# Building an expert gate table by one-hot matmuls, or by indirect DMA of single elements

## The chip, the cores and the metric

The kernel runs on one core of one Trainium2 chip. The metric is the device time of one execution in microseconds (us). The engines are PE (TensorE, with its weight loads shown apart as PEld), DVE (VectorE), ACT (ScalarE), POOL (GpSimd) and SP (SyncE, which here only issues DMAs).

## The reference

Two transformer blocks are applied to 512 tokens of width 1024, all in float32. The part that matters is the last one, a feed-forward layer over 16,384 experts of one neuron each. For each token and each of 8 heads, two lists of 128 key scores are ranked, the best 16 of each are crossed, and the best 16 of the 256 sums name 16 experts. A softmax over the 16 gives the gates.

```python
s1, i1 = lax.top_k(s[:, :, 0], PEER_TOPK)
s2, i2 = lax.top_k(s[:, :, 1], PEER_TOPK)
cand = (s1[..., :, None] + s2[..., None, :]).reshape(...)
cidx = (i1[..., :, None] * PEER_NKEYS + i2[..., None, :]).reshape(...)
cs, ci = lax.top_k(cand, PEER_TOPK)
eidx = jnp.take_along_axis(cidx, ci, axis=-1)
g = jax.nn.softmax(cs, axis=-1)
hid = jnp.einsum('cd,chkd->chk', xc, ug).astype(jnp.float32)
a = jax.nn.gelu(hid, approximate=False) * g
return jnp.einsum('chk,chkd->cd', a.astype(vg.dtype), vg)
```

A token can pick the same expert in several heads; its gates then add up.

## The kernel before, in words

The program is written by hand: each engine has one instruction stream, and semaphores tie the streams together. The first half of it computes the two attention blocks. The change is in the expert layer, which has two stages.

**Hidden stage.** The 16,384 experts are walked as 128 tiles of 128 experts. For tile e, SP loads a 512 KB weight tile (`load_u`, four slots). Products are made in three passes of a split float32: ACT writes the high part of the weights (`high_u`, two slots), POOL subtracts it from the weights to get the low part (`low_u`), and PE multiplies high by high, high by low and low by high: 24 matmuls of 512 columns per tile (`hidden`). ACT applies gelu (`kept_tile`), and SP stores the result in HBM; the last 32 tiles stay on chip (`on_chip_tile`). `high_u(e+2)` waits until PE is done with tile e, so the low part of tile e+2 can be made only while PE works on tile e+1.

**Ranking.** In the same stage DVE ranks the experts of four blocks of 128 tokens (`retrieve(tb)`). The first three blocks (`DENSE = 3`) are treated as dense: all 16,384 experts are evaluated for them, and a gate table `gates[key 1][key 2][token]` in HBM holds a gate, mostly zero, for each expert and token. The fourth block fetches its own rows and elements by indirect DMA in the next stage (`row_gather`, `element_gathers`, 128 of each, on POOL).

**The gate table before.** For each dense block PE transposes the ranked lists (`lists_out`), DVE builds one-hot matrices for each token (`onehots`), PE multiplies them so that a 128 by 128 table per token comes out (`gate_group`, 8 matmuls of 128 columns put into the middle of each of 16 tiles per block), ACT copies it to SBUF (`copy_group`), and SP stores it (`store_gates`, 8 DMAs of 1024 KB per block). `FREE` and `START` say which tiles have no gate work.

**Output stage.** For each tile SP loads values, gates and kept hidden units; DVE multiplies gates and hidden units (`gated`), and PE adds up the outputs (`outputs`, 18 matmuls per tile).

Of the kernel before, what the change touches and what calls it, by code (L numbers as in the profile page):

```python
# [21 lines left out]
F32 = mybir.dt.float32  # L22
F32R = mybir.dt.float32r
BF16 = mybir.dt.bfloat16
U32 = mybir.dt.uint32
# [5 lines left out]
P = 128  # L31
# [19 lines left out]
FREE = (8, 7, 7)  # L51
GATED = 16
START = [sum(FREE[:i]) + GATED * i for i in range(DENSE + 1)]
# [285 lines left out]
def program(nc, t_in, out):  # L339
    build_schedule()  # L340
    ctx = ExitStack()
    with ctx:
# [41 lines left out]
        row_no = region(o + TD, P).bitcast(U32)  # L384
        hidden_no = region(o + T + TD, P).bitcast(U32)
        row_gate = region(o + 2 * T + TD, P)
# [61 lines left out]
        ohring = rt(10240, 2 * 2 * 4 * P).rearrange("p (s w u i) -> p s w u i", s=2, w=2, u=4)  # L448
# [15 lines left out]
        stage = staged[:, :].rearrange("p (i t) -> p i t", i=P)  # L464
# [4 lines left out]
        token = rt(20112, 1)  # L469
# [49 lines left out]
        s_init = sem("buffers_set")  # L519
        s_init2 = sem("second_block_buffers_set")  # L520
# [47 lines left out]
        s_lt = sem("lists_transposed")  # L568
        s_ltc = sem("lists_copied")
        s_hx = sem("residual_transposed")  # L570
        s_hxc = sem("residual_copied")
        s_oh = sem("onehots_ready")
        s_gm = [sem(f"gate_groups_done_bank{i}") for i in range(2)]
        s_ge = [sem(f"gate_groups_copied_bank{i}") for i in range(2)]
        s_gst = sem("gates_stored")
# [115 lines left out]
        def _(sp):  # L691
# [60 lines left out]
            def store_gates(tb, parts):  # L752
                for c in parts:
                    sp.dma_start(gates[16 * c:16 * c + 16, :, tb * P:(tb + 1) * P].rearrange("i j t -> j i t"),
                                 stage[:, 16 * c:16 * c + 16, :]).then_inc(s_gst, 16)

            PIECES = [[0], [1], [2, 3], [4, 5], [6, 7]] + [[]] * 3

# [3 lines left out]
            for tb in range(DENSE):  # L762
                for i in range(FREE[tb]):
                    if tb:
                        store_gates(tb - 1, PIECES[i])
                    tile(START[tb] + i)

                def gated_tiles(it, _):
                    for u in range(4):
                        tile(it * 4 + (START[tb] + FREE[tb] + u), (START[tb] + FREE[tb] + u) % 4)  # L770
                rounds(sp, GATED // 4, gated_tiles)
                for u in range(2):
                    sp.wait_ge(s_ge[u], 16 * (tb + 1))
            for i, e in enumerate(range(START[DENSE], NS)):
                if i < len(PIECES):
                    store_gates(DENSE - 1, PIECES[i])
                tile(e)
# [36 lines left out]
        def _(pool):  # L814

            nc.gpsimd.memset(zc[:, 0:T + 2], 0.0).then_inc(s_init, 1)
# [50 lines left out]
            def low_u(e, slot):  # L867
                pool.wait_ge(s_uhi, e + 1)
                nc.gpsimd.tensor_tensor(U2[:, slot % 2, 1].rearrange("p k e -> p (k e)"), UR[:, slot, :],  # L869
                                        U2[:, slot % 2, 0].rearrange("p k e -> p (k e)").bitcast(F32),  # L870
# [1155 lines left out]
```

## Time and profile before

| | us |
|---|---|
| median of 3 runs (2627.72 to 2630.12) | 2629.23 |
| the profiled execution, its own time | 2629.53 |
| its span, first to last instruction | 2627.7 |
| PE busy | 2453.8 |
| DVE busy | 1319.6 |
| ACT busy | 1060.0 |
| POOL busy | 929.8 |

The span is the stretch that the trace covers. A busy time is a sum over the span, so it says nothing yet of which engine is waited for at a given place. That is read from the stretches and chains below.

### The profile page before, as it was taken

Reading aid. Unit: us, or ns where it says so; the run is one execution under the profiler, and the core shown is the slowest. Engines: PE = TensorE matmul, PEld = TensorE weight load, DVE = VectorE, ACT = ScalarE, POOL = GpSimd, SP = SyncE. Lnnn points to the kernel's source line nnn. Section 1 sums busy time; section 2 is a strip of 40 time slices with the busy share of each in tenths; the row PEclk is TensorE's granted clock in tenths of the full one; section 3 lists DMA queues with packets and bytes.
Section 4 is the critical chain, followed back from the end, with each engine's and each line's share of the span. In section 5 each row is a group of like instructions: output and inputs, shape, how many; then the busy total and the mean of one; then the engine's idle time right before and its main releaser. Section 6 shows DMA issues by size and latency. Waiting matters only on the chain.

```text
span 2627.7 us, 32392 instructions
## 1 busy us (share of the span) xinstructions
PE 2453.8 (93%) x10455; PEld 1851.9 (70%) x10455; DVE 1319.6 (50%) x2863; ACT 1060.0 (40%) x1532; POOL 929.8 (35%) x536
## 2 busy tenths in 40 slices
PE   7888788799998899889999999999999999999997
PEld 5544444578873555468888888887888788888886
DVE  1444422232221234527977868773000198888886
ACT  4564574433323344433345454442222243333333
POOL 2211100244430112123333434334444465555553
PEclk9999898999999899899999999999999999999998
DMA  3111011123321111022233837447443499999995
GB/s 142 60 41 36 28 45 63 44 73 97 98 90 48 65 33 41 25 80 92 81 117 108 248 108 221 145 132 237 144 126 108 166 323 332 353 354 352 354 356 212
DMA packets 199729, 379.79 MB, mean 145 GB/s; under 512 B 21424, under 2 KB 129968, under 8 KB 199376
## 3 DMA queue, kind: packets, MB, share of 16 engines
q1 hardware_dynamic: 176592, 311.31, 36.3%
q0 software_dynamic: 23040, 67.22, 7.0%
q8 instruction: 57, 0.93, 0.1%
q14 instruction: 40, 0.33, 0.0%
HBM read 323.91 MB, written 54.53 MB: 144 GB/s over the span
## 4 chain that ended last, share of the span: by engine, by line
PE 43%; issue 15%; POOL 6%; ACT 1%; DVE 1%; DMA 0%; POOLq 0%; DVEq 0%; ACTq 0%
PE bank L1168 19%; PE bank L1157 10%; PE bank L948 8%; POOL u_split L869 6%; PE bank L1077 2%; PE bank L1048 1%; PE bank L1113 1%; PE bank L1061 1%; ACT u_split L1287 0%; ACT blocks L1378 0%; PE bank L1001 0%; ACT blocks L1271 0%; DMA tail<-hidden_of_last_block,low 0%; DVE low L1586 0%; DVE h_low L1608 0%
## 5 line engine op out<-in xcount | busy, mean ns | idle before, releaser
L1157 PE MATMUL bank<-h_high,u_split 128*128 128x512 f32 x2048 | 659.9, 395 | 10.0 <-POOL u_split L869 8.8
L829 POOL TENSOR_TENSOR u_split<-blocks,u_split 128x1024 fp32r<-128x1024 f32 x106 | 256.7, 2422 | 948.4 <-ACT u_split L1287 947.8
L948 PE MATMUL bank<-h_high,u_split 128*128 128x512 f32 (+1 forms) x1696 | 565.3, 406 | 24.8 <-DVE h_low L1608 13.6
L1168 PE MATMUL bank<-v_split,a_split 128*128 128x512 f32 x2304 | 524.3, 390 | 3.2 <-DVE a_split L1858 3.2
L1168 PEld LDWEIGHTS bank<-v_split,a_split 128*128 128x128 f32 x2304 | 433.5, 188 | 93.8 <-DVE v_split L1855 3.6
L869 POOL TENSOR_TENSOR u_split<-tail,u_split 128x1024 fp32r<-128x1024 f32 x128 | 326.2, 2549 | 483.0 <-ACT u_split L1439 483.0
L1157 PEld LDWEIGHTS bank<-h_high,u_split 128*128 128x128 f32 x2048 | 385.5, 188 | 91.0 <-POOL u_split L869 8.9
L948 PEld LDWEIGHTS bank<-h_high,u_split 128*128 128x128 f32 (+1 forms) x1696 | 326.7, 193 | 117.6 <-issue 31.7
L1157 PE MATMUL bank<-h_low,u_split 128*128 128x512 f32 x1024 | 399.6, 390 | 0.0
L948 PE MATMUL bank<-h_low,u_split 128*128 128x512 f32 x720 | 286.7, 398 | 0.0
L1855 DVE TENSOR_TENSOR v_split<-tail,v_split 128x1024 fp32r<-128x1024 f32 x128 | 158.5, 1238 | 232.0 <-ACT v_split L1492 232.0
L1492 ACT CAST v_split<-tail 128x1024 fp32r<-128x1024 f32 x128 | 134.9, 1054 | 298.3 <-PE bank L1168 297.6
L1823 DVE TENSOR_SCALAR tail<-low 128x128 f32<-128x128 f32 x384 | 194.8, 507 | 104.8 <-PE bank L1144 94.7
L1157 PEld LDWEIGHTS bank<-h_low,u_split 128*128 128x128 f32 x1024 | 193.1, 189 | 36.3
L876 POOL DMA_INDIRECT low<-in_v,low x128 | 131.5, 1027 | 179.8 <-DVE low L1874 147.9
L884 POOL DMA_INDIRECT tail<-hidden_of_last_block,low x128 | 167.9, 1312 | 43.9 <-issue 38.7
L1456 ACT COPY staged<-bank 128x512 f32 (+1 forms) x96 | 104.5, 1093 | 153.9 <-PE bank L1144 153.9
L1874 DVE SCALAR_TENSOR_TENSOR low<-low,tail 128x1024 f32<-128x1024 f32 x128 | 163.5, 1277 | 0.8 <-DVE tail L1864 0.4
L948 PEld LDWEIGHTS bank<-h_low,u_split 128*128 128x128 f32 x720 | 139.1, 193 | 32.4 <-issue 5.4
L1048 PE MATMUL bank<-blocks 96*128 96x512 f32 (+3 forms) x224 | 101.5, 565 | 49.3 <-DVE blocks L1644 20.0
L1439 ACT CAST u_split<-tail 128x1024 fp32r<-128x1024 f32 x128 | 133.0, 1040 | 18.9 <-DMA tail<-in_uT 13.5
L1444 ACT ACTIVATE tail<-bank 128x512 f32<-128x512 f32 x96 | 57.5, 599 | 184.8 <-PE bank L1157 184.8
(210 smaller groups left out, 2740.6 us busy)
## 6 DMA issues: line engine op xcount, KB each, us to landing
tail<-in_uT SPq DMA_DIRECT2D x128, 512.0 KB, 3.7
tail<-in_v SPq DMA_DIRECT2D x128, 512.0 KB, 5.8
gates<-staged SPq DMA_DIRECT2D x24, 1024.0 KB, 7.3
tail<-gates SPq DMA_DIRECT2D x128, 192.0 KB, 5.6
kept_hidden<-tail SPq DMA_DIRECT2D x96, 192.0 KB, 1.9
tail<-kept_hidden SPq DMA_DIRECT2D x96, 192.0 KB, 5.8
blocks<-in_r SPq DMA_DIRECT2D x24, 512.0 KB, 3.5
blocks<-in_conv SPq DMA_DIRECT2D x16, 512.0 KB, 3.3
```

Of the source, the lines that this page charges most:

```text
L829: nc.gpsimd.tensor_tensor(flat(u, 1)[:, 0:n], ring[:, loads[0] % NW, 0:n], flat(u, 0)[:, 0:n].bitcast(F32), ALU.subtract).then_inc(s_wlo, 1)
L869: nc.gpsimd.tensor_tensor(U2[:, slot % 2, 1].rearrange("p k e -> p (k e)"), UR[:, slot, :], U2[:, slot % 2, 0].rearrange("p k e -> p (k e) ...
L876: nc.gpsimd.indirect_dma_start(rows_in[:, k % 4, :], None, v_rows, bass.IndirectOffsetOnAxis(ap=row_no[:, k:k + 1], axis=0))\
L884: nc.gpsimd.indirect_dma_start(picked[:, k:k + 1], None, hidden_elements, bass.IndirectOffsetOnAxis(ap=hidden_no[:, k:k + 1], axis=0))\
L948: last = mm(ps[0:m, :], flat(u, part)[:, k * m:(k + 1) * m], x, start=(k == 0 and j == 0), stop=(k == nk - 1 and j == 2))
L1157: last = mm(bank[slot % 2][:, :], U2[:, slot % 2, w, k, :], x[:, k, :], start=(k == 0 and x is hh and w == 0), stop=(k == KD - 1 and w == 1))
L1168: done = mm(bank[2 + 2 * tb + dh][:, :], A2[:, slot, wa, tb * P:(tb + 1) * P], V2[slot // 2][:, slot % 2, wv, dh * T:(dh + 1) * T], start= ...
L1439: nc.scalar.copy(U2[:, slot % 2, 0].rearrange("p k e -> p (k e)"), UR[:, slot, :]).then_inc(s_uhi, 1)
L1492: nc.scalar.copy(V2[slot // 2][:, slot % 2, 0], VR[:, slot, :]).then_inc(s_vhi, 1)
L1823: V.tensor_scalar(ohring[:, u, 0, k, :], iota, lists[:, 0, bass.ds(t + k, 1)], lists[:, 2, bass.ds(t + k, 1)], ALU.is_equal, ALU.mult)
L1855: V.tensor_tensor(V2[slot // 2][:, slot % 2, 1], VR[:, slot, :], V2[slot // 2][:, slot % 2, 0].bitcast(F32), ALU.subtract).then_inc(s_vlo, 1)
L1874: V.scalar_tensor_tensor(sparse, rows_in[:, slot, :], rated[:, bass.ds(k, 1)], sparse, ALU.mult, ALU.add).then_inc(s_axpy, 1)
```

## The change

The one-hot matmuls, their copies and the stores of the table go. In their place:

- POOL clears a buffer of zeros at the start of the program, and SP writes it 32 times over the gate table, one DMA behind each of 32 weight loads of the first block.
- DVE turns the ranked lists into element numbers, and POOL adds each gate into the table by an indirect DMA with an add: one DMA for each of 128 ranks of a dense block (128 elements each, one per token), 384 in all. The 16 ranks of a head go out together; the next head of the same block waits until they have landed, since it may name the same experts. The blocks are interleaved, two heads apart.
- POOL no longer makes the low parts of the expert weights. DVE makes them, between the steps of `retrieve`, one per tile; `retrieve` is a generator that yields eight times.
- SP loads the first gates of the output stage at tile 124, behind a wait for all 384 scatters.

```diff
+            def zero_gates(c):
+                sp.dma_start(gates[4 * c:4 * c + 4].rearrange("i p t -> p i t"),
+                             zeros.rearrange("p (i t) -> p i t", i=4)).then_inc(s_zero, 16)
+            sp.wait_ge(s_zset, 1)
             for L in range(len(LOADS)):
                 weights(L)
+                if NW <= L < NW + NKEYS // 4:
+                    zero_gates(L - NW)
...
-            sp.wait_ge(s_gst, 128 * DENSE)
-            for e in range(4):
-                load_gates(e, NS + e, e)
+            rounds(sp, NS // 4, lambda it, _: [tile(it * 4 + u, u) for u in range(4)])
             for e in range(NS, NT):
+                if e == NT - 4:
+                    for tb in range(DENSE):
+                        sp.wait_ge(s_sc[tb], 16 * P)
+                    for q in range(4):
+                        load_gates(q, NS + q, q)
...
+            def scatter_head(tb, h):
+                if h == 0:
+                    pool.wait_ge(s_tk, tb + 1)
+                else:
+                    pool.wait_ge(s_sc[tb], 16 * TOPK * h)
+                for k in range(TOPK * h, TOPK * (h + 1)):
+                    nc.gpsimd.indirect_dma_start(gate_elements,
+                                                 bass.IndirectOffsetOnAxis(ap=expert_no[tb][:, k:k + 1], axis=0),
+                                                 expert_gate[tb][:, k:k + 1], None, compute_op=ALU.add)\
+                        .then_inc(s_sc[tb], 16)
+            for i in range(PEER_HEADS + 2 * (DENSE - 1)):
+                for tb in range(DENSE):
+                    if 0 <= i - 2 * tb < PEER_HEADS:
+                        scatter_head(tb, i - 2 * tb)
...
-                    if between and k % 4 == 2:
-                        between(k // 4)
...
+            rounds(pe, NT // 4, lambda it, _: [hidden(it * 4 + u, u) for u in range(4)], first=True)
...
+            def low_u(e, slot):
+                dve.wait_ge(s_uhi, e + 1)
+                V.tensor_tensor(U2[:, slot % 2, 1].rearrange("p k e -> p (k e)"), UR[:, slot, :],
+                                U2[:, slot % 2, 0].rearrange("p k e -> p (k e)").bitcast(F32),
+                                ALU.subtract).then_inc(s_ulo, 1)
...
+            low_u(0, 0)
+            low_u(1, 1)
+            for tb in range(TB):
+                for i, _ in enumerate(retrieve(tb)):
+                    low_u(LOWS * tb + i + 2, (LOWS * tb + i + 2) % 4)
```

Where the instructions move is shown at three places. On POOL, behind the last low part of the `wq` weights (the row with x24), the program before goes on with the low parts of the expert weights (L869, the middle four in a loop), and then with the gathers of the output stage:

```order
L829 TENSOR_TENSOR u_split<-blocks,u_split 128x1024 x24
L869 TENSOR_TENSOR u_split<-tail,u_split 128x1024 x2
L682 UNCONDITIONAL_BRANCH
L682 ISA
L869 TENSOR_TENSOR u_split<-tail,u_split 128x1024
...
L869 TENSOR_TENSOR u_split<-tail,u_split 128x1024 x2
L876 DMA low<-in_v,low 128x1024 x4
L884 DMA tail<-hidden_of_last_block,low 128x1 x8
```

The same place after the change:

```order
L814 TENSOR_TENSOR u_split<-blocks,u_split 128x1024 x24
L874 DMA gates<-low 6291456x1 x384
L855 DMA low<-in_v,low 128x1024 x4
L863 DMA tail<-hidden_of_last_block,low 128x1 x8
```

POOL has 384 scatters where it had 128 subtractions, and the gathers of the fourth block stand behind them.

On DVE, behind the ranking of the last key scores (L1738), the program before runs one `retrieve` without a break:

```order
L1738 MAX_INDEX tail<-tail 128x8 x4
L1777 TENSOR_TENSOR tail<-tail 128x2048
L1779 CAST tail<-tail 128x256
L1781 MAX tail<-tail 128x8 x8
L1784 MAX_INDEX tail<-tail 128x8 x8
L1787 MATCH_REPLACE tail<-tail 128x256 x8
L1790 MAX tail<-tail 128x8 x8
L1793 MAX_INDEX tail<-tail 128x8 x8
```

After the change the low parts (L1708) of tiles 0 and 1 come first, and one stands behind each step:

```order
L1708 TENSOR_TENSOR u_split<-tail,u_split 128x1024 x2
L1718 TENSOR_TENSOR tail<-tail 128x2048
L1720 CAST tail<-tail 128x256
L1722 MAX tail<-tail 128x8 x8
L1708 TENSOR_TENSOR u_split<-tail,u_split 128x1024
L1726 MAX_INDEX tail<-tail 128x8 x8
L1708 TENSOR_TENSOR u_split<-tail,u_split 128x1024
L1730 MATCH_REPLACE tail<-tail 128x256 x8
L1708 TENSOR_TENSOR u_split<-tail,u_split 128x1024
```

The two low parts that open the stage have moved from POOL, where nothing was ahead of them, to DVE, behind the ranking.

On SP, at the last four tiles of the hidden stage, the queue is after the change (with what each row waits for):

```order
L725 DMA tail<-in_uT 128x1024 [waits u_low_parts]
L747 DMA tail<-gates 128x384 [waits gates_scattered_block2,gates_scattered_block1,gates_scattered_block0]
L747 DMA tail<-gates 128x384 x3
L742 DMA tail<-in_v 128x1024 [waits u_low_parts]
L770 DMA hidden_of_last_block<-staged 128x128 [waits gelu_done]
```

Everything from the second row on, the first values of the output stage among it, stands behind the last scatter; all weight tiles of the hidden stage stand ahead of it.

## Rows read from the trace of the kernel before

**Rows 1.** Stretches: length, busy us (x) of PE, PEld, DVE, ACT, POOL, clock, DMA, GB/s.

```profile
1332.00:1441.00 109.00, 109.00 (x603) 94.54 (x602) 76.67 (x241) 55.96 (x61) 35.92 (x15) 1.00 0.35 109
1806.00:2083.00 277.00, 273.45 (x1199) 225.97 (x1198) 6.23 (x7) 79.48 (x104) 119.69 (x50) 0.99 0.42 130
1283.90:2083.90 800.00, 789.43 (x3850) 663.80 (x3851) 410.72 (x1133) 318.18 (x375) 322.38 (x127) 1.00 0.49 151
2083.90:2627.70 543.80, 524.15 (x2304) 433.18 (x2303) 439.73 (x547) 193.11 (x265) 299.42 (x256) 0.98 0.92 328
```

**Rows 2.** The chain of waits: start us, us, what the time went to.

```profile
1349.47 4.82 issue
1354.32 2.40 POOL u_split L869
...
1809.94 273.97 PE bank L1157 x1200
```

**Rows 3.** Groups by line: the matmuls of the hidden stage.

```profile
L1157 PE MATMUL bank<-h_high,u_split 128*128 128x512 f32 x2048 | 659.9, 395 | 10.0 <-POOL u_split L869 8.8 <-ACT low L1463 1.2
```

**Rows 4.** DVE in order of time, one ranking: start us, length, line.

```profile
1288.67 2.27 DVE L1777 TENSOR_TENSOR tail<-tail 128x2048 f32<-128x2048 f32 x1
...
1294.06 0.09 DVE L1784 MATCH_VALUE_LOAD tail<-tail 128x8 f32 x1
...
1297.35 0.09 DVE L1787 MATCH_VALUE_LOAD tail<-tail 128x8 f32 x1
...
1300.63 2.71 DVE L1790 MAX8 tail<-tail 128x8 f32<-128x256 f32 x8
1303.38 0.09 DVE L1793 MATCH_VALUE_LOAD tail<-tail 128x8 f32 x1
...
1306.67 0.29 DVE L1798 TENSOR_TENSOR tail<-tail 128x128 f32<-128x128 f32 x1
...
1314.12 2.29 DVE L1812 TENSOR_REDUCE tail<-tail 128x128 f32<-128x2048 f32 x1
1316.44 0.23 DVE L1804 TENSOR_SCALAR tail<-tail 128x128 uint32<-128x128 uint32 x1
...
1323.93 0.29 DVE L1814 TENSOR_REDUCE tail<-tail 128x8 f32<-128x128 f32 x1
```

**Rows 5.** ACT in order of time: gelu of a tile, then a high part.

```profile
1295.07 0.60 ACT L1444 ACTIVATE tail<-bank 128x512 f32<-128x512 f32 x1 [3.90 <-PE bank L1157]
1295.57 1.04 ACT L1439 CAST u_split<-tail 128x1024 fp32r<-128x1024 f32 x1
```

**Rows 6.** Two lines of DVE: shortest, median and longest duration in ns.

```profile
L1811 DVE TENSOR_TENSOR tail<-tail x8: 2292/3324/4370, 1309.7 to 1786.7; 128x2048 f32<-128x2048 f32 x8
L1855 DVE TENSOR_TENSOR v_split<-tail,v_split x128: 1210/1225/2577, 2075.6 to 2596.1; 128x1024 fp32r<-128x1024 f32 x128
```

**Rows 7.** PE in order of time: in brackets the wait just before.

```profile
2103.42 21.87 PE L1168 MATMUL bank<-v_split,a_split 128*128 128x512 f32 x88 [3.21 <-DVE a_split L1858]
```

**Rows 8.** The stretch just behind it; columns as in rows 1.

```profile
2104.50:2108.50 4.00, 4.00 (x12) 3.17 (x11) 4.00 (x6) 1.73 (x3) 3.39 (x3) 0.57 0.68 222
```

**Rows 9.** DMAs issued by POOL: all element gathers (ns), one in time, one plain DMA.

```profile
L884 POOL DMA_INDIRECT tail<-hidden_of_last_block,low x128: 941/1328/1686, 2091.2 to 2589.1; - x128
...
2094.91 0.94 POOL L884 DMA_INDIRECT tail<-hidden_of_last_block,low  x1 [0.30 <-issue]
...
1031.52 0.52 POOL L839 DMA_DIRECT2D blocks<-in_bias  x1
```

**Rows 10.** DVE's first instruction behind a group of element gathers.

```profile
2100.85 0.16 DVE L1864 TENSOR_TENSOR tail<-tail,low 128x4 f32<-128x4 f32 x1 [11.58 <-DMA tail<-hidden_of_last_block,low]
```

**Rows 11.** DMA issues: count, KB each, median us from issue to landing.

```profile
tail<-in_v SPq DMA_DIRECT2D x128, 512.0 KB, 5.8
gates<-staged SPq DMA_DIRECT2D x24, 1024.0 KB, 7.3
...
hidden_of_last_block<-staged SPq DMA_DIRECT2D x32, 64.0 KB, 1.5
```

More of the change, by code:

```diff
@@ L50 @@
 TD = DENSE * P
-FREE = (8, 7, 7)
-GATED = 16
-START = [sum(FREE[:i]) + GATED * i for i in range(DENSE + 1)]
+LOWS = 8
 NS = 96
@@ L383, in program @@
         lists = region(o, 3 * T, 3)
[L384 to L386 removed]
+        expert_no = [region(o + 2 * P * tb, P).bitcast(U32) for tb in range(TB)]
+        expert_gate = [region(o + 2 * P * tb + P, P) for tb in range(TB)]
+        row_no = expert_no[DENSE]
+        row_gate = expert_gate[DENSE]
+        hidden_no = region(o + 2 * P * TB, P).bitcast(U32)
         o += 3 * T + 2
@@ L463, in program @@
         assert TAIL + 19856 <= SB
-        stage = staged[:, :].rearrange("p (i t) -> p i t", i=P)
+        zeros = region(HH + 6144, 4 * TD)
         on_chip = staged[:, :].rearrange("p (e t) -> p e t", e=NL)
@@ L814, in _ @@
         def _(pool):
+            nc.gpsimd.memset(zeros, 0.0).then_inc(s_zset, 1)
             nc.gpsimd.memset(zc[:, 0:T + 2], 0.0).then_inc(s_init, 1)
@@ L1126, in _, with hidden @@
             pe.wait_ge(s_hxc, 2)
-            def lists_out(tb):
-                if tb == 0:
-                    pe.wait_ge(s_hxc, 8)
-                pe.wait_ge(s_tk, tb + 1)
-                if tb >= 1:
-                    pe.wait_ge(s_ltc, tb)
-                for w in range(3):
-                    last = nc.tensor.transpose(bank[4][:, w * P:(w + 1) * P], sel[:, w, :], ident)
-                last.then_inc(s_lt, 1)
-            def gate_group(n, u):
-                pe.wait_ge(s_oh, n * 2 + (u + 1))
-                at_least(pe, s_ge[u], n)
-                for k in range(4):
-                    last = mm(bank[2 + u][:, k * P:(k + 1) * P], ohring[:, u, 1, k, :], ohring[:, u, 0, k, :],
-                              start=True, stop=True)
-                last.then_inc(s_gm[u], 1)
-            def hidden(e, slot, between=None):
+            def hidden(e, slot):
                 pe.wait_ge(s_ulo, e + 1)
@@ L1829, in _ @@
-            for tb in range(DENSE):
-                retrieve(tb)
-                dve.wait_ge(s_ltc, tb + 1)
-                rounds(dve, P // 8, lambda it, _: [
-                    onehots(it + 16 * tb, u, it * 8 + (P * tb + 4 * u)) for u in range(2)], first=tb == 0)
-            def gather_lists():
-                number = cbf[:, 0, :]
-                dve.wait_ge(s_tk, TB)
-                link(V.tensor_tensor(number, ident, iota, ALU.mult))
-                link(V.tensor_reduce(token, number, AX.X, ALU.add))
-                link(V.scalar_tensor_tensor(number, sel[:, 0, :], float(NKEYS), sel[:, 1, :], ALU.mult, ALU.add))
-                V.tensor_copy(row_no, number).then_inc(s_ix, 1)
-                link(V.tensor_scalar(cbf[:, 1, :], number, float(P), token, ALU.mult, ALU.add))
-                V.tensor_copy(hidden_no, cbf[:, 1, :]).then_inc(s_ix, 1)
-                V.tensor_copy(row_gate, sel[:, 2, :]).then_inc(s_ix, 1)
-                dve.wait_ge(s_ix, 3)
@@ L1848, in _ @@
-            retrieve(DENSE)
-            gather_lists()
+            dve.wait_ge(s_kb[3], 16 * 4)
+            link(V.tensor_tensor(cbf[:, 0, :], ident, iota, ALU.mult))
+            link(V.tensor_reduce(token[:, 0:1], cbf[:, 0, :], AX.X, ALU.add))
+            for tb in range(1, DENSE):
+                ins = V.tensor_scalar(token[:, tb:tb + 1], token[:, 0:1], float(P * tb), None, ALU.add)
+            link(ins)
+            low_u(0, 0)
[3 more added lines that the diff above has]
+                    low_u(LOWS * tb + i + 2, (LOWS * tb + i + 2) % 4)
@@ L1851, in gated @@
+            low_u(TB * LOWS + 2, 2)
+            low_u(TB * LOWS + 3, 3)
+            with dve.Fori(TB * LOWS // 4 + 1, NT // 4) as it:
+                for u in range(4):
+                    low_u(it * 4 + u, u)
             def gated(j, it, slot, hid):
```

133 lines of the change are left out of this document (39 added, 94 removed).

## The prediction

> **What bounds the kernel now.** I first cut the span at the start and the end of the hidden stage. It runs from the first matmul of tile 0 at 1283.9 to 2083.9, 800.0 us, and PE is busy in 789 of them; the output stage and the ending take 543.8 more [rows 1]. Then the stage's matmuls: over all 128 tiles they waited 10.0 us [rows 3]. So PE is what the stage waits for, and the question is what PE does there. The two inner stretches answer it. In the last one only the 24 matmuls of a tile are left, and the chain of waits gives 273.97 us for 1200 matmuls [rows 2], 50 tiles at **5.48 us**. In the first one PE does gate matmuls too, 603 instructions in 109 us [rows 1], and the chain repeats every 4.82 + 2.40 = 7.2 us [rows 2]. The reader is to see that POOL's name in that chain is no sign of a slow POOL: the low part follows PE's end of a tile, and PE is full all the while.
>
> **What the change takes away.** The gate matmuls, transposes and their waits leave PE's queue. What is left is 128 x 5.48 = 701.4 us, so 800.0 - 701.4 = **98.6 us** less. ACT and SP lose copies and stores that nobody waited for by themselves: ACT was busy 318 of 800 us, DMA 0.49 [rows 1].
>
> **The start of the stage.** DVE ends the ranking of the key scores at 1288.67, where `retrieve` begins [rows 4]. The low part of tile 0 now stands behind that. Three short instructions come first (0.95 us, an estimate from 0.3 us for L1798, which has the same 128x128 shape [rows 4]), then the low part. That operation on DVE is L1855's, two SBUF inputs of 128x1024: median 1.225 us [rows 6], 1.26 with its gap. PE starts at 1288.67 + 0.95 + 1.26 = 1290.9, **7.0 us** later than now.
>
> **Low parts between the ranking steps.** From tile to tile the low part may start when PE has ended tile e, ACT has run gelu and the high part (1295.07 to 1296.61, 1.54 us [rows 5]) and three semaphores have passed, 0.1 each by the gaps between the engines: 1.9 us after PE's end. It must be done when PE ends tile e+1. From the starts in [rows 4] the eight steps are 5.39 (1294.06 - 1288.67), 3.29, 3.28, 3.05 (2.75 and the 0.3 of L1798), 3.29, then 5.17 (1314.12 - 1306.88, L1798's end, without the 2.07 us by which its L1811 is over the shortest one of 2.29 [rows 6]), 2.32 and 7.49. The tail of a ranking (sums, reciprocal, gates, element numbers) is six or seven instructions of L1798's size or less, 1.8 us. With low parts that is 35 + 10 = 45 us of DVE for eight tiles of 5.48 = 43.8: DVE is just full, which no share of the page says. Written out tile by tile, PE waits only behind the two long steps: the last step of a ranking (7.49) makes one tile 1.0 us late, and the tail with the next first step (7.2) the next one 3.0 us. Three times both and once the first: **12.8 us**.
>
> The waits have a second price. Behind the one wait of 3.2 us that PE has now [rows 7] the granted clock was 0.57 over the next 4 us [rows 8], so partly at 1.2 and not 2.4 GHz, which costs 4 x 0.43 = 1.7 us. The later start and the three 3.0 us waits may each do that: 4 x 1.7 = **6.8 us**, or nothing, if the wait must be as long as that one.
>
> **The scatters.** POOL's 384 scatters start when the first gates are ready: by the same account eight tiles into the stage, at 1343. No row shows an indirect DMA that adds. The nearest is the element gather, also 128 elements of 4 bytes with one index each: 0.94 us at its shortest, median 1.33, at most 1.69, and 0.30 between two [rows 9]. In the output stage DVE is busy 440 of 544 us [rows 1], and there the median is what counts: 1.62 us from start to start. I take that for the 96 scatters that fall in the rankings, and 1.40 for the other 288, where DVE only has a low part in each 5.5 us and stretches one scatter in three. Waits for landings that nothing covers: the first two heads and the last two, and the end, five of 5.0 us (the fourth gather ends on POOL at 2094.91 + 0.94 = 2095.85, DVE goes on at 2100.85 [rows 9, 10]). Sum: 96 x 1.62 + 288 x 1.40 + 25 = 584, so the last has landed at **1927**.
>
> When is that too late? The hidden stage ends at 1290.9 + 701.4 + 12.8 + 6.8 = 2011.9. SP comes to the gates at tile 124, about 1990. Behind the last scatter stand the loads of values (5.8 us [rows 11]), their high and low part and the products, about 9 us, so no harm is done before 2003. The scatters have 76 us, or **0.20 us each**, to spare. From there on every 0.1 us per scatter costs 38 us.
>
> What can the adding cost? From below: nothing; the gather's row stands as it is. From above: a plain DMA of POOL takes 0.52 [rows 9], so 0.42 of the 0.94 belongs to the 128 elements. If a third access per element adds as much again, it is +0.42; if everything doubles, +0.94. I take 0 as likeliest, since source, index and target are the same in number as in the gather, and keep both ends.
>
> On the DMA side 128 elements are 8 for each of 16 engines. A store of 512-byte pieces took 7.3 us for 2048 of them [rows 11], 57 ns for each piece on an engine; the budget is 660 us over 3072 elements, 0.21 us each. That is nearly four times the row.
>
> **The zeros.** 32 stores of 768 KB, estimated from 1024 KB in 7.3 us [rows 11] at 5.5 us each, behind weight loads that are asked for five loads ahead. I cost them at 0; the cover is those four projections in between, some 20 us, and without it one store would cost up to 5.5. In the output stage nothing moves.
>
> **A rule against it.** Gathers follow each other 1.25 us apart while their data takes 5 us to land [rows 9, 10], so POOL does not wait for each. The Trainium skill, "DMA: Bandwidth & Descriptors", section on the anatomy of a DMA on the gpsimd path, puts a fixed 2.0 us on each such DMA, mostly the receipt of the write. By that, if they ran one behind the other, the scatters would take 768 us, and the total would be near 2665. The trace's spacing does not agree with such a chain for gathers; no run here shows it for writes.
>
> **The sum** is made against the profiled execution's 2629.5, 0.3 over the median: 2629.5 - 98.6 + 7.0 + 12.8 + 6.8 = **2557.5**. Without waits and clock it is 2538. If each step is 1 us longer, since POOL's descriptor work holds DVE up as it now did L1811 (2.29 to 4.37 [rows 6]), the same tile by tile account gives 31.3 us of waits, 2576; with 2 us on each step 2608.
>
> **The rivals.**
> - *The adding scatter is dear to issue*, and POOL becomes the bound. For it: 384 in one queue, and only 0.20 us to spare. Against: the gather's row. Between +0.20 and +0.38 the change still gains, 2560 to 2629. At +0.385 the scatters land at 2075 and nothing is left; that is the point that decides. At +0.42 it is 1927 + 161 = 2088, outputs start at 2097 in place of 2083.9: 2643. At +0.94: 2843.
> - *Landings in a chain.* If each add had to land before the next is begun, at 1.5 us, which a 64 KB store of 128 rows takes [rows 11], beside 1.25 to issue: 384 x 2.75, end at 2399, total 2954.
> - *DVE is the bound* in the first 34 tiles: 2576 to 2608 as above.
> - *Nothing changes*, because scatters end by chance near 2075.
>
> **Chances.** Forecast 0.50 (its own range 2537 to 2580), partly late scatters 0.07, DVE 0.06; dear issue past the turning point 0.26, landings or DMA engines 0.07; the same 0.04. A measurement here tells 0.2%, 5 us, from no change. So faster 0.63, same 0.04, slower 0.33. The range reaches from 2537 to 2700: above it lie the costlier half of the dear issue and most of the landings, 0.17, below it 0.02.
>
> **What would show it.** A hidden stage of 2012 - 1291 = 721 us with 24 matmuls per tile and 5.48 us between gelus; waits of PE for DVE's low part at tiles 9 and 10, 17 and 18, 25 and 26; the scatters 1.25 to 1.6 us apart and over near 1927, SP not waiting for them. I am wrong if the scatters are 1.85 us apart or more, if POOL waits long between heads in the middle of the stage, or if the first block's projections wait for weights.

## The result and the profile after

The change makes the kernel slower by 1%, a small loss but clear of the noise. Before takes 2629.68 us (median of 4 executions), after 2653.80 (median of 4, 2653.51 to 2664.95). The ratio is 1.0101, with a 95% interval of 1.0072 to 1.0129. The prediction was 2557, faster.

The profiled execution of after is the slowest of its four, 2664.95 us, span 2663.1. It reaches the hidden stage 7 to 13 us later than the profiles of the experiments below whose first low part is on VectorE as well (1303.3 against 1290.2 to 1296.2), so positions in it are read with that shift in mind. Durations and distances aren't touched by it.

The groups by line, with busy us, mean ns, idle us before and what ended it:

```profile
L874 POOL DMA_INDIRECT gates<-low x384 | 625.2, 1628 | 201.2 <-issue 116.3 <-DVE low L1773 77.9 <-DMA gates<-low 7.0
L1126 PE MATMUL bank<-h_high,u_split 128*128 128x512 f32 x2048 | 635.6, 391 | 18.4 <-DVE u_split L1708 18.4
```

The first row answers to nothing in before: 384 scatters hold POOL for 625 us, and 116 more lie between them. The second answers to [rows 3]: the matmuls of the hidden stage still hardly wait, 18.4 us, now for DVE. Three stretches (columns as in [rows 1]) show what that gained and where it was lost:

```profile
1303.30:2015.90 712.60, 702.39 (x3072) 578.65 (x3072) 289.72 (x460) 204.73 (x264) 551.73 (x337) 0.99 0.61 130
1500.00:2000.00 500.00, 500.00 (x2207) 414.00 (x2207) 113.44 (x95) 139.93 (x183) 418.73 (x265) 1.00 0.64 134
2000.00:2130.00 130.00, 24.63 (x97) 19.76 (x96) 11.01 (x14) 10.71 (x15) 94.11 (x64) 0.58 0.33 52
```

The hidden stage is down from 800.0 us [rows 1] to 712.6, and in its middle PE is full. But behind it comes a hole that before did not have: PE works 24.6 of 130 us, while POOL is busy for 94. The list of waits names it (us in total, times, longest):

```profile
ACT v_split L1428 <- DMA tail<-in_v: 112.3, 3, 111.8
...
PE bank L1137 <- DVE a_split L1800: 105.4, 1, 105.4
DVE tail L1795 <- DMA tail<-gates: 104.3, 1, 104.3
```

```profile
SPq L763 <- DMA gates<-low: 112.4, 1, 112.4
```

The last row is SP's own queue: it stands 112.4 us before the scatters' semaphores (L763), and the first gates and values of the output stage stand behind. PE, DVE and ACT all wait for these, one wait of over 100 us each. POOL in order of time, the first three scatters, and the shortest, median and longest of all:

```profile
1358.08 2.82 POOL L874 DMA_INDIRECT gates<-low  x1 [77.87 <-DVE low L1773]
1361.20 1.56 POOL L874 DMA_INDIRECT gates<-low  x1 [0.30 <-issue]
1363.06 2.04 POOL L874 DMA_INDIRECT gates<-low  x1 [0.30 <-issue]
```

```profile
L874 POOL DMA_INDIRECT gates<-low x384: 1544/1546/3370, 1358.1 to 2105.0; - x192
```

The shortest adding scatter takes 1.54 us, where the shortest element gather takes 0.94 [rows 9]. With 0.30 between two that is 1.85 from start to start at best. From the first to the last start it is 2105.0 - 1358.1 = 746.9 us for 383 distances, **1.95 each**. The chain of waits near its end has nothing else in it:

```profile
2101.32 1.55 POOL gates L874
2102.86 0.30 issue
2103.17 1.55 POOL gates L874
2104.71 0.30 issue
2105.02 3.01 DMA gates<-low
```

### The profile page after: what moved, and what is told of

It reads as the page before. It is cut to its first block, busy times and chain, and to the rows that moved or that the text cites. A ratio compares the mean times of both kernels' runs of the same rounds, so it can differ in the third digit from the quotient of the medians.

```text
span 2663.1 us, 29585 instructions
## 1 busy us (share of the span) xinstructions
PE 2377.6 (89%) x9678; PEld 1771.9 (67%) x9678; DVE 1210.2 (45%) x2233; ACT 954.6 (36%) x1433; POOL 1240.0 (47%) x793
## 4 chain that ended last, share of the span: by engine, by line
PE 34%; POOL 23%; issue 5%; DVE 2%; ACT 1%; DMA 1%; SPq 0%; DVEq 0%; ACTq 0%; POOLq 0%
POOL gates L874 23%; PE bank L1137 20%; PE bank L940 8%; PE bank L1069 2%; PE bank L1126 2%; PE bank L1040 1%; DMA gates<-low 1%; PE bank L1053 1%; PE bank L1105 1%; ACT u_split L1241 0%; ACT blocks L1332 0%; PE bank L993 0%; DMA tail<-in_v 0%; ACT blocks L1225 0%; DVE low L1520 0%
## 5 line engine op out<-in xcount | busy, mean ns | idle before, releaser
L874 POOL DMA_INDIRECT gates<-low x384 | 625.2, 1628 | 201.2 <-issue 116.3
L1126 PE MATMUL bank<-h_high,u_split 128*128 128x512 f32 x2048 | 635.6, 391 | 18.4 <-DVE u_split L1708 18.4
L1708 DVE TENSOR_TENSOR u_split<-tail,u_split 128x1024 fp32r<-128x1024 f32 x128 | 156.8, 1226 | 412.8 <-ACT u_split L1395 409.9
L855 POOL DMA_INDIRECT low<-in_v,low x128 | 141.4, 1105 | 163.6 <-DVE low L1816 139.4
L1395 ACT CAST u_split<-tail 128x1024 fp32r<-128x1024 f32 x128 | 133.0, 1040 | 0.0
L1585 DVE TENSOR_REDUCE low<-bank 128x1 f32<-128x512 f32 (+3 forms) x112 | 59.9, 537 | 116.0 <-PE bank L1042 58.8
```

Of the source, the lines that this page charges most:

```text
L855: nc.gpsimd.indirect_dma_start(rows_in[:, k % 4, :], None, v_rows, bass.IndirectOffsetOnAxis(ap=row_no[:, k:k + 1], axis=0))\
L874: nc.gpsimd.indirect_dma_start(gate_elements, bass.IndirectOffsetOnAxis(ap=expert_no[tb][:, k:k + 1], axis=0), expert_gate[tb][:, k:k + 1] ...
L1126: last = mm(bank[slot % 2][:, :], U2[:, slot % 2, w, k, :], x[:, k, :], start=(k == 0 and x is hh and w == 0), stop=(k == KD - 1 and w == 1))
L1395: nc.scalar.copy(U2[:, slot % 2, 0].rearrange("p k e -> p (k e)"), UR[:, slot, :]).then_inc(s_uhi, 1)
L1708: V.tensor_tensor(U2[:, slot % 2, 1].rearrange("p k e -> p (k e)"), UR[:, slot, :], U2[:, slot % 2, 0].rearrange("p k e -> p (k e)").bitca ...
```

## The experiments

The theory after the result: POOL's time to issue is the bound, and the add is what makes it dear. Rivals: the writes' landing or the DMA engines set the pace, or the rest of the forecast was wrong as well. All versions are edits of after. Where a version writes without adding and sums nothing beforehand, a token that picks an expert in two heads keeps one of its gates and not the sum. The two versions with half of the scatters, or half of the elements in each, leave half of the gates out of the table. These two, the two paced ones and the repeat of after were executed once each, the others 4 to 10 times.

### Plain writes in place of adding ones

```diff
-                                                 expert_gate[tb][:, k:k + 1], None, compute_op=ALU.add)\
+                                                 expert_gate[tb][:, k:k + 1], None)\
```

> The 384 scatters write their elements without adding (where two heads of a token name one expert, only one gate stays in the table); queue, waits and all else as in the changed kernel. Theory A, the add is what costs POOL its time: an issue falls from 1.55 us to the gather's 0.94 at its shortest, start to start from 1.85 to 1.25, the last scatter lands about 384 x 0.61 = 234 us earlier, near 1875, ahead of the end of the hidden stage, so PE no longer waits for gates: about 2555 us. Theory B, it is the scattered writing to HBM that costs (index on the target side): still 1.55 and 2654 us. Theory C, landings fill the queue: spacing falls little, and the waits between heads stay.

Measured: 2913.56 us, ratio to before 1.1073 (1.1055 to 1.1092). The issue is as cheap as a gather's:

```profile
L874 POOL DMA_INDIRECT gates<-low x384: 952/958/2495, 1349.5 to 1880.9; - x192
```

So the add costs 1.545 - 0.955 = **0.59 us** of POOL per scatter. With plain writes POOL was done at 1882, early enough, and the kernel was still 260 us slower than after. The stretches:

```profile
1500.00:1540.00 40.00, 33.19 (x134) 25.57 (x133) 9.66 (x14) 7.66 (x10) 29.68 (x30) 0.94 0.35 106
1540.00:1600.00 60.00, 15.18 (x31) 8.25 (x30) 1.23 (x1) 1.53 (x2) 45.67 (x48) 0.56 0.06 14
1600.00:1700.00 100.00, 18.67 (x34) 9.58 (x33) 1.23 (x1) 1.53 (x2) 75.91 (x80) 0.52 0.04 8
1880.00:2000.00 120.00, 93.16 (x394) 75.56 (x394) 20.84 (x17) 26.73 (x36) 1.53 (x2) 0.86 0.36 111
```

When the scatters reach their full rate of 80 in 100 us, 1.26 us apart, the hidden stage all but stops: PE does 34 matmuls in 100 us, and SP's queue moves 8 to 14 GB/s in place of 106, one weight tile in 67 us. The expectations below call this starved loads, but it is not the loads that are waited for. Here are PE and ACT in order of time, SP's three issues for a tile, and a stretch around the load:

```profile
1672.87 0.59 PE L1126 MATMUL bank<-h_low,u_split 128*128 128x512 f32 x1 [2.21 <-issue]
1675.67 0.59 PE L1126 MATMUL bank<-h_high,u_split 128*128 128x512 f32 x1 [2.21 <-issue]
...
1646.25 0.60 ACT L1400 ACTIVATE tail<-bank 128x512 f32<-128x512 f32 x1 [65.67 <-remote]
1646.75 1.04 ACT L1395 CAST u_split<-tail 128x1024 fp32r<-128x1024 f32 x1
1713.48 0.60 ACT L1400 ACTIVATE tail<-bank 128x512 f32<-128x512 f32 x1 [65.70 <-remote]
...
1647.01 0.33 SPq L730 DMA_DIRECT2D kept_hidden<-tail  x1
1651.82 0.69 SPq L732 DMA_DIRECT2D hidden_of_last_block<-tail  x1
1655.33 0.70 SPq L725 DMA_DIRECT2D tail<-in_uT  x1
...
1654.00:1656.50 2.50, 0.52 (x1) 0.19 (x1) 0.00 (x0) 0.00 (x0) 1.89 (x3) 0.92 0.63 210
```

The load moves at 210 GB/s as soon as SP asks for it, and ACT makes the next high part (L1395) right behind the gelu, without a wait for a weight tile. What is slow is PE: most of its matmuls start 2.8 us apart, and the trace shows nothing that they wait for ("issue"). The 67.2 us of a tile are 24 x 2.8, though the record has the first ten of the 24 closer together and then 20 us of nothing before the gelu. The waits of ACT, 66 us each, are put down to nothing that the profile can name ("remote"), and SP needs 8 us for three issues that take it 1 us elsewhere. SP asks for so few loads because the tiles end so late. PE goes on at this pace for 12 us behind the last scatter, idles, and is full again from 1910. I had not expected that, and it needs a theory of its own: the rate of the writes, or the plain write as such. Two experiments below tell them apart.

### Half of the scatters

```diff
-            for i in range(PEER_HEADS + 2 * (DENSE - 1)):
+            for i in range(PEER_HEADS // 2 + 2 * (DENSE - 1)):
```

(and the same half in the condition below it and in SP's wait).

> Only the first four heads of each dense block are scattered, 192 adding DMAs in place of 384 (half of the gates are missing from the table). If POOL's queue of scatters is the only thing that made the changed kernel slow, the queue ends near 1358 + 192 x 1.95 = 1730, long before the hidden stage, and the time is what I forecast for a hidden queue: 2550 to 2560 us, with 12 to 19 us of waits of PE for DVE's low parts. If something else holds the stage up, it stays above 2600.

Measured: 2547.96 us. The 192 scatters run from 1345.0 to 1732.3, so nobody waits for them, and the hidden stage runs from 1290.2 to the start of its last matmul at 2002.4, the 712.6 us of after. This is the forecast's world with the queue out of the way; the rest of the forecast stands.

### The first head of each block by plain writes

The first head of a block finds zeros and names 16 different experts, so its writes need no add.

```diff
-                                                 expert_gate[tb][:, k:k + 1], None, compute_op=ALU.add)\
+                                                 expert_gate[tb][:, k:k + 1], None,
+                                                 **({"compute_op": ALU.add} if h else {}))\
```

> The 48 scatters of the first head of each block write without adding (the table is zero there, so the result is the same), the other 336 add. Theory A (the add costs 0.61 us of issue): 48 x 0.61 = 29 us less than the changed kernel, 2625 us, level with the kernel before. Theory B: no change, 2654.

Measured: 2632.0 us, ratio 1.000 (0.999 to 1.001): an eighth of the adds less brings the kernel back to before. The last scatter starts at 2071.3. The expectation was 7 us lower. The stall of the plain writes shows here too, in small: where the 16 plain scatters of the third block follow each other 1.26 us apart, PE waits for nothing that is shown, and the clock falls.

```profile
1600.00:1700.00 100.00, 90.82 (x380) 72.84 (x379) 19.19 (x16) 24.52 (x32) 82.94 (x57) 0.93 0.59 125
```

The hidden stage takes 731 us and not 713. The time does not show it, since POOL's queue ends later still.

### Half of the elements in each scatter

```diff
-                                                 bass.IndirectOffsetOnAxis(ap=expert_no[tb][:, k:k + 1], axis=0),
-                                                 expert_gate[tb][:, k:k + 1], None, compute_op=ALU.add)\
+                                                 bass.IndirectOffsetOnAxis(ap=expert_no[tb][0:P // 2, k:k + 1], axis=0),
+                                                 expert_gate[tb][0:P // 2, k:k + 1], None, compute_op=ALU.add)\
```

> Each of the 384 adding DMAs scatters 64 elements (the first 64 tokens of a block; the others' gates are missing) in place of 128. If the issue is a fixed part of 0.52 us, as of a plain DMA, and the rest by the element: 0.52 + 1.03 / 2 = 1.04 us in place of 1.55, start to start 1.34, and the queue ends before the hidden stage: about 2555. If the cost is by the DMA: still 1.55 and 2654.

Measured: 2617.02 us.

```profile
L874 POOL DMA_INDIRECT gates<-low x384: 1404/1409/2664, 1346.0 to 2058.4; - x192
```

64 elements take 1.405 us and 128 take 1.545: 2.2 ns for an element and, if it goes by a straight line, about 1.26 that don't depend on their number. The expectation of 1.04 us was wrong. Most of the price of an adding scatter is one per DMA, and so is most of the add's part of it: if the 0.59 us went by the element, half of them would have saved 0.30 for the add alone, and they saved 0.14 in all. So fewer DMAs would help more than smaller ones.

The pages count the packets of the queue that carries POOL's DMAs (packets, MB, share of the 16 engines), in before, after, the plain version and this one:

```profile
q0 software_dynamic: 23040, 67.22, 7.0%
q0 software_dynamic: 78336, 67.45, 12.7%
q0 software_dynamic: 35328, 67.45, 6.7%
q0 software_dynamic: 53760, 67.35, 12.2%
```

Less the 23,040 of the gathers, that is 144 packets for each adding scatter, 32 for each plain one and 80 for one that adds 64 elements: an add moves each element by itself. At the 2.2 ns by which POOL's time grows for each of them, 112 packets more are 0.25 us of the 0.59, an estimate; what the rest is stays open.

### Plain writes, further apart

One GpSimd memset behind each plain scatter, into a buffer that is free then. The second of the two experiments has the four added lines twice.

```diff
+                    if sets[0]:
+                        pool.wait_ge(s_pace, sets[0])
+                    nc.gpsimd.memset(pace, 0.0).then_inc(s_pace, 1)
+                    sets[0] += 1
```

> The kernel after with plain element writes in place of adding ones (as in the plain scatter, experts that a token picks in two heads keep one gate instead of the sum), and behind each of the 384 scatters one GpSimd memset of 128 x 256 elements into a buffer that is free then (a 128 x 514 one takes 0.53 us and a 128 x 1 one 0.11, so about 0.3 us). That stretches the spacing of scatters from 1.26 us to about 1.65. Theory A (at 1.26 us the element writes take nearly all the time of the DMA engines, and SyncE's loads starve; the adding itself keeps them apart): spaced out, the loads get through, the hidden stage is back at 712 to 725 us, the scatters end near 1350 + 634 = 1984, before they are waited for: 2555 us (2545 to 2600). Rival B (it is the plain writes as such that hold the queues up, whatever their spacing, because an adding DMA is split or ordered in another way): the loads stay 60 us apart through the scatters and the time stays over 2850 us. Rival C (the spacing is not enough): in between, 2600 to 2850, with the loads of the hidden stage slowed in proportion.

> The same with two such memsets behind each scatter: spacing about 1.26 + 2 x 0.35 = 1.95 us, which is that of the adding scatters. Theory A: the hidden stage is undisturbed and the scatters end as late as with adding, 1350 + 749 = 2099: about 2630 to 2655 us, the time of the kernel after, though nothing is added. That would show that the number of us per issue on GpSimd alone makes the loss, not anything in memory. Rival B: over 2850 us again.

Measured: **2553.39** us with one memset, 2635.18 with two. With one, POOL in order of time and two stretches:

```profile
1353.54 0.98 POOL L878 DMA_INDIRECT gates<-low  x1 [0.17 <-issue]
1354.51 0.34 POOL L884 MEMSET tail<- 128x256 f32 x1
1355.01 0.96 POOL L878 DMA_INDIRECT gates<-low  x1 [0.16 <-issue]
```

```profile
1500.00:1600.00 100.00, 100.00 (x443) 82.83 (x442) 22.33 (x18) 27.60 (x36) 88.65 (x126) 1.00 0.50 147
1600.00:1700.00 100.00, 100.00 (x443) 82.84 (x442) 22.68 (x19) 29.15 (x38) 89.31 (x130) 1.00 0.48 143
```

The distance is 1.47 us (my 1.65 was too much, since only 0.17 lies between a scatter and what follows it here), and the loads run at 143 to 147 GB/s with PE full. So 1.26 us apart all but stops the hidden stage, and 1.47 us apart does nothing to it. It is the rate, not the plain write. It is not the number of packets either, since after moves 144 for each scatter and its PE is full. With two memsets the scatters are nearly as slow as adding ones (1.90 us apart, from 1350.7 to 2078.4), and 2635 us come back although nothing is added: POOL's time per scatter alone makes the loss, and nothing in memory is needed for it.

### Low parts of the first tiles on GpSimd

In the version with the first heads plain, GpSimd makes the low parts of tiles 0 to 9 before its first scatter, and VectorE ranks block 0 without a break.

```diff
+            for e in range(LOWS + 2):
+                pool.wait_ge(s_uhi, e + 1)
+                nc.gpsimd.tensor_tensor(U2[:, e % 2, 1].rearrange("p k e -> p (k e)"), UR[:, e % 4, :], ...
...
-            low_u(0, 0)
-            low_u(1, 1)
-            for tb in range(TB):
+            for _ in retrieve(0):
+                pass
+            dve.wait_ge(s_ulo, LOWS + 2)
+            for tb in range(1, TB):
```

> The kernel with plain writes for the first head of each block and adding ones for the rest (2632.0 before), and in it GpSimd, which is idle then, makes the low parts of the expert weights of tiles 0 to 9; VectorE ranks block 0 without a break, ScalarE's exponentials of block 0 come at tile 5 instead of 7. Theory A (the end is set by GpSimd's queue of scatters, so an earlier start shows one for one): the hidden stage starts about 7 us sooner, since its first low part is no longer behind VectorE's key ranking, and the first gates are ready about 45 instead of 54 us into the stage: the scatters start 10 to 17 us sooner and the kernel takes 2615 to 2622 us. Rival B (GpSimd's 2.42 us for a low part of 1024 elements, on the path from a loaded tile to its matmuls, against VectorE's 1.2): the first tiles wait, and the gain is under 4 us, 2628 or more.

Measured: 2621.73 us, ratio 0.9963 (0.9949 to 0.9976), 10.3 us less than without it. The first scatter starts at 1336.5 in place of 1348.0, the last at 2065.8 in place of 2071.3 in the profiled executions. An earlier start shows, and the time is at the upper end of the expected 2615 to 2622. Of the 11.5 us by which the first scatter is earlier the last one keeps 5.5 in the profiles; that this was lost beside VectorE's work on the next block (see the last section) was not tested.

### Sums on VectorE, plain writes everywhere

If every copy of an expert in a token's list carries the sum, no add is needed. VectorE builds the sums in 16 groups of 8 picks per block, one group between two low parts.

```diff
+                for c in range(SUMS):
+                    link(V.tensor_tensor(m3, number[:, 8 * c:8 * c + 8].unsqueeze(2).to_broadcast([P, 8, P]),
+                                         number.unsqueeze(1).to_broadcast([P, 8, P]), ALU.is_equal))
+                    link(V.tensor_tensor(m3, m3, single.unsqueeze(1).to_broadcast([P, 8, P]), ALU.mult))
+                    ins = V.tensor_reduce(expert_gate[tb][:, 8 * c:8 * c + 8], m3, AX.X, ALU.add)
...
+                    yield
```

With it come the memset behind each scatter, GpSimd's low parts of tiles 0 to 17 and larger offsets of the blocks.

> A version that computes everything: VectorE sums, for each token and each of its 128 picks, the gates of all picks with the same expert (16 groups of 8 picks in each of three blocks: compare, multiply, reduce on 128 x 1024 elements, about 3.5 us a group, one group between two low parts), so that duplicates carry the same total and plain writes can replace the adding ones; one GpSimd memset of 128 x 256 elements behind each scatter keeps them 1.46 us apart and more; GpSimd makes the low parts of tiles 0 to 17, and the blocks follow each other later (offsets of 0, 5 and 8 heads). Theory A (issue time of GpSimd decides, plus room for SyncE's loads; VectorE has room for 16 x 3.5 us a block): first scatter near 1385 to 1400, 384 x 1.5 us and some 20 to 30 us of landing waits, last one before 2030, the hidden stage at 712 to 725 us from about 1284: 2545 us (2538 to 2570). Rival (VectorE becomes the bound of the tiles, 3.5 + 1.2 us of work a tile and more against PE's 5.45): the stage is stretched by some 0.3 us in each of 48 tiles or more, 2560 to 2600 us.

Measured: 2613.42 us, ratio 0.9936 (0.9922 to 0.9950), 68 us over the expectation.

```profile
L881 POOL DMA_INDIRECT gates<-low x384: 964/967/2431, 1408.2 to 2053.8; - x192
```

```profile
L1143 PE MATMUL bank<-h_high,u_split 128*128 128x512 f32 x2048 | 634.6, 391 | 32.3 <-DVE u_split L1728 30.7 <-ACT low L1430 1.2 <-POOL u_split L893 0.5
```

The scatters wait for the sums of block 0, start at 1408.2 and end at 2053.8, 24 us later than expected. The other 44 us are the expectation's own: it took an end at 2030 to be early enough, and by the table in the next section each us after some 1990 counts. PE waits 32.3 us for low parts and the hidden stage takes 733, so the rival came about as well, behind the later end of the queue. Then the same with block 0, whose gates are ready first, left to the adding scatters (and with GpSimd's low parts of tiles 0 to 9 alone):

```diff
-                if tb == DENSE:
+                if tb in (0, DENSE):
...
-                                                 expert_gate[tb][:, k:k + 1], None)\
+                                                 expert_gate[tb][:, k:k + 1], None,
+                                                 **({} if tb or not h else {"compute_op": ALU.add}))\
```

> The last version's scatters ended at 2045 us, and each us after about 2003 is lost: they began at 1400, behind the sums of block 0. Here block 0, whose gates are the first to be ready, is scattered by adding (its first head by plain writes) without sums, so scatters begin near 1337 as with the low parts of tiles 0 to 9 on GpSimd; blocks 1 and 2 are summed on VectorE (plain writes with one memset behind each), at offsets of 4 and 8 heads. Everything is computed. Sum: 112 x 1.9 + 272 x 1.5 = 621 us and about 8 landing waits of 3 us: last scatter near 1337 + 645 = 1982 to 1995. Theory A (GpSimd's queue decides): 2550 us (2543 to 2570), with VectorE's 32 more groups of 3.7 us stretching the hidden stage by 5 to 10 us. Rival (VectorE becomes the bound): the hidden stage is over 735 us and the time over 2575.

Measured: **2582.42** us, ratio 0.9814 (0.9799 to 0.9830). It leaves nothing out and beats both kernels.

```profile
L881 POOL DMA_INDIRECT gates<-low x384: 963/967/3083, 1337.5 to 2024.2; - x192
```

The end is at 2024 and not at 1995, so 30 us of the expected gain are missing, nearly all in the queue; the hidden stage was not stretched (PE waited 6.8 us in it).

### After, profiled once more

> The kernel after, profiled once more. Its first profile starts the expert stage 12.4 us later than the kernel before did, and that execution took 2665 us where the three others took 2653.5. Theory A (the 12.4 us belong to that one execution, not to the change): this one takes 2653 to 2655 us, the hidden stage starts near 1291, the scatters end near 2092. Rival (the 32 stores of zeros at the start cost it): the stage starts again near 1303.

Measured: 2664.48 us, the stage from 1302.1, the scatters to 2104.4. So the late stage came in both profiled executions of this very program, and is not one odd execution. The stores of zeros don't explain it: all experiments have them and start at 1288 to 1296. Between 795 and 888 us the granted clock was 0.91 in both profiles of after and 0.94 in the one with half of the scatters, whose instructions there are the same, and 16 matmuls fewer were done. Why this program's profile meets a lower clock there stays open; of the 35 us between the profile of after and that of before it is 12, while the median of after is free of it if the 11 us between 2664.95 and 2653.8 are the same 12.

## Why the prediction was wrong

**The step that failed** is "What can the adding cost? ... I take 0 as likeliest", and with it the term 96 x 1.62 + 288 x 1.40 + 25 = 584 us. Measured are 746.9 us from the first start to the last and 3.0 for the last landing, 750. The add costs 0.59 us per scatter, between the two bounds that the prediction gave (+0.42 and +0.94), and past its own turning point of +0.385. The rival "the adding scatter is dear to issue", with 0.26, is what happened, with the mechanism, the place (SP's wait at tile 124, POOL's queue ahead of it) and, partly by luck, nearly the price: 2643 at +0.42. At the measured +0.59 the prediction's own account gives a landing at 1927 + 227 = 2154 and some 2709 us. That it was less is the rest of the term: the waits for landings took 10 us and not 25, and the plain scatters took 531 from first to last and not 559. The argument that source, index and target are the same in number as in the gather was an argument about the transfer; that the row of a gather says nothing on what GpSimd does for an add was known, and with bounds on both sides of the turning point the value at the lower bound had no row behind it.

**The turning point held.** Over the profiled executions of nine kernels, with the start of the last scatter and the time (worked out from the results and from groups as above):

```
version                     last scatter     time   difference
half of the scatters              1732.3   2547.96     815.7
plain, one memset                 1970.6   2553.39     582.8
two blocks summed                 2024.2   2583.26     559.1
summed, all plain                 2053.8   2613.16     559.4
half of the elements              2058.4   2617.02     558.6
first tiles on GpSimd             2065.8   2625.73     559.9
first heads plain                 2071.3   2631.19     559.9
plain, two memsets                2078.4   2635.18     556.8
after                             2105.0   2664.95     560.0
```

The plain scatters without a memset are not in it, since there the hidden stage itself is stretched; the repeat of after is at 560.1. Seven of the nine end 557 to 560 us after their last scatter, whatever else they do, and the two whose last scatter starts before 1971 don't. The two take 2548 and 2553, and the line of the others comes to that at 1989 to 1994; no version ended between 1971 and 2024. So past some 1990 each us of the queue is one of the kernel, a little earlier than forecast ("no harm is done before 2003"), and the time of before is met at 2629.5 - 559.5 = 2070, against a forecast of 2075.

**The rest of the sum**, by the version with half of the scatters: 2548.0 against 2557.5.

- The hidden stage took 712.6 us, forecast 721. PE's 128 tiles are 702.4 us busy against 128 x 5.48 = 701.4: the 98.6 us are there.
- Its start: 1290.2 against 1290.9. In after the steps are the forecast ones (0.87 us from the end of the key ranking to the first low part, which takes 1.2):

```profile
1301.04 0.27 DVE L1777 TENSOR_TENSOR tail<-low 128x128 f32<-128x128 f32 x1
1301.34 0.29 DVE L1778 TENSOR_REDUCE tail<-tail 128x1 f32<-128x128 f32 x1
1301.66 0.21 DVE L1780 TENSOR_SCALAR tail<-tail 128x1 f32<-128x1 f32 x2
1301.91 2.36 DVE L1708 TENSOR_TENSOR u_split<-tail,u_split 128x1024 fp32r<-128x1024 f32 x2
```

- Waits of PE for low parts: forecast 12.8 us, by waits of 1.0 and 3.0 at the end of each ranking. Measured 18.4 with the one before the stage's first matmul, which is 8.2, so 10.2 within the stage; the first four are 0.71, 2.47, 0.70 and 2.43.
- Why less: the prediction feared that POOL's descriptor work holds DVE up. It does not here. The instruction that is L1811 in before is L1755 in after, and it takes the same time eight times over, six of them beside the scatters. In before POOL made no DMA in the stage, only subtractions, so the 4.37 of [rows 6] came from something else.

```profile
L1755 DVE TENSOR_TENSOR tail<-tail x8: 2291/2292/2293, 1338.7 to 1492.9; 128x2048 f32<-128x2048 f32 x8
```

- Clock: forecast 6.8 us. The granted clock was 0.51 in the first 5.0 us of the stage, 12 matmuls where the full clock gives 22, and 0.97 in 50 us around the wait of 2.43:

```profile
1303.30:1308.30 5.00, 5.00 (x12) 3.93 (x13) 4.93 (x8) 0.00 (x0) 0.00 (x0) 0.51 0.00 0
```

  That is 2.3 + 1.5, some 4 us, an estimate; the wait of 2.47 shows no such fall (1.00 from 1350 to 1400). The sum of 702.4 is only 1.0 above 701.4 because the 5.48 us had a lower clock in it too (0.99 in the second stretch of [rows 1]); from 1500 to 2000 a tile takes 5.44.
- The first gates: forecast 52 us into the stage, measured 54.8 (first start at 1358.1, behind 1303.3).
- Landings: forecast 25 us, measured 7.0 in 4 waits and 3.0 at the end.

**The rule against it.** In the trace the scatters of a head start 1.85 us apart while the last one takes 3.0 us to land, so the landing of one lies beside the issue of the next; from start to start they took 1.26 us without the add, and 1.71 with half of the elements. The Trainium skill, "DMA: Bandwidth & Descriptors", section on the anatomy of a DMA on the gpsimd path, puts a fixed 2.0 us on each such DMA, mostly the receipt of the write. One behind the other, that would make 768 us of the queue, an estimate, and 750 were measured. The two are near each other by chance: no run here shows the scatters of a head waiting for one another's receipt.

The rival of landings in a chain (2954 us) and that of VectorE as the bound did not come about. The time of the plain scatters, 2914, is near the first of these, but for a reason that no rival had.

## What to carry to other kernels

When work is moved into one long queue, divide its slack by the number of entries first (here 0.20 us for each of 384), and if the price of one entry has bounds on both sides of that figure, the likeliest value is not the lower bound; it is unknown, and the forecast belongs in the middle. Where the last entry of a queue gates a stage, look at the start of the last entry in each version: here one number explains the times of all the versions that wait for it. An accumulate in an indirect DMA costs GpSimd 0.59 us here, most of it once for each DMA; where duplicates can be summed beforehand, plain writes of equal values do the same, but they need room between them. And where a stage slows down, look at who waits for whom before calling it bandwidth: few GB/s can mean that few loads were asked for.

## What was unexpected of the hardware

- An indirect scatter of 128 elements of 4 bytes takes GpSimd 0.955 us and moves 32 packets; when it adds, it is 1.545 us and 144 packets. Half of the elements save only 0.14.
- Adding scatters were slower still beside a busy VectorE, whose own instructions did not get longer. GpSimd and VectorE in after, the same length of time during the rankings and after them:

```profile
1400.00:1450.00 50.00, 46.86 (x200) 38.03 (x199) 44.62 (x92) 15.15 (x19) 41.49 (x24) 0.97 0.62 135
1550.00:1600.00 50.00, 50.00 (x222) 41.41 (x221) 11.91 (x10) 13.80 (x18) 41.26 (x27) 1.00 0.67 146
```

  With VectorE busy for 44.6 of 50 us GpSimd issues 24 scatters, with 11.9 it issues 27: 2.08 against 1.85 us each (2.01 without the one wait of 1.8 for a landing). In the version with two blocks summed, VectorE's sums run beside them. Its 112 x 1.85 + 272 x 1.47 = 607 us of shortest distances became 687 with 17.5 of landing waits, so about 62 us lie in longer ones. That VectorE's work is the cause was not tested apart.
- Plain scatters of 4-byte elements 1.26 us apart slow TensorE down to one matmul in 2.8 us, ScalarE and SyncE along with it, while a weight load still moves at 210 GB/s; 16 of them in a row are enough to see it, and at 1.47 us apart they cost nothing. In the stalled stretch the DMA engines show a share of 0.04 to 0.06, so their recorded time is not what is used up. What is, and where between 1.26 and 1.47 us the edge lies, stays open.
